# Attention of a two-layer encoder: three groups in rounds, value columns as weights, sums that come out transposed

## The reference

```python
# a: latent attention, head width 96 for q and k, 64 for v
p = softmax(q @ k.T * 96**-0.5);  o = p @ v
# b: windowed attention, +-128 tokens, a sink logit per head
e = exp(s - m); p = e / (sum(e) + exp(sink - m)); o = p @ v
# c: two maps of width 32 per head
p1 = softmax(q1 @ k1.T * 32**-0.5);  p2 = softmax(q2 @ k2.T * 32**-0.5)
o = (p1 - lam * p2) @ v
o = rms_norm(o, norm_g) * (1 - lambda_init)
x = x + g1 * (concat(a, b, c, d) @ w_out)
```

## Time and profile before

| | |
|---|---|
| median of 3 runs | 1745.44 us (1743.79 to 1755.22) |
| the profiled execution | 1747.51 us |
| its span in the trace | 1745.7 us |
| PE busy | 1387.3 us (79%) |
| DVE, ACT, POOL busy | 618.0, 369.3, 265.9 us |
| attention stage, layer 0 | 314.64 to 480.61 us |
| attention stage, layer 1 | 1145.35 us to some 166 us later |

### The profile page before, as it was taken

How to read it: one execution, slowest core, us unless ns; L and a number is a source line. 1 busy time by engine, 2 the same in 40 slices (tenths; PEclk the granted TensorE clock), 3 DMA queues, 4 the chain that set the end, 5 groups by cost and what they waited for, 6 DMA issues and landing times.

```text
span 1745.7 us, 18431 instructions
## 1 busy us (share of the span) xinstructions
PE 1387.3 (79%) x6748; PEld 787.5 (45%) x6748; DVE 618.0 (35%) x1444; ACT 369.3 (21%) x832; POOL 265.9 (15%) x250
## 2 busy tenths in 40 slices
PE   2789999898696768878778999988869778877841
PEld 0245646565443434444324465656544344444421
DVE  3461523358624212221136152335861431111111
ACT  0211111545402101111021111154530211111101
POOL 0000301000001333333200030100000134333311
PEclk9789999999898779999978999999989879999986
DMA  7611120441334499999961113045124449999942
GB/s 234 253 51 48 72 88 10 155 179 44 127 123 157 180 295 408 407 406 402 360 226 63 48 51 109 2 146 191 49 104 146 157 158 386 403 401 401 398 141 109
DMA packets 98152, 335.53 MB, mean 192 GB/s; under 512 B 28310, under 2 KB 33046, under 8 KB 72816
## 3 DMA queue, kind: packets, MB, share of 16 engines
q1 hardware_dynamic: 74688, 305.48, 44.8%
q0 software_dynamic: 15072, 16.85, 4.2%
q10 hardware_dynamic: 8304, 12.03, 2.0%
HBM read 324.04 MB, written 27.80 MB: 202 GB/s over the span
## 4 chain that ended last, share of the span: by engine, by line
PE 63%; DVE 13%; issue 9%; ACT 7%; DMA 4%; POOL 2%; SPq 1%; POOLq 0%; DVEq 0%; ACTq 0%
PE bank L458 57%; ACT pr_r L1212 2%; DMA big<-in_ada_w_dram 2%; PE bank L706 2%; PE bank L804 2%; DVE pr_r L1679 1%; DVE pr_r L1818 1%; DVE pr_r L1821 1%; ACT pr_r L1259 1%; DVE pr_r L1544 1%; PE bank L790 1%; PE bank L556 1%; POOL small L1319 1%; ACT ht_r L1191 1%; SPq L917 1%
## 5 line engine op out<-in xcount | busy, mean ns | idle before, releaser
L458 PE MATMUL bank<-big,pr_r 128*64 128x256 f32 (+2 forms) x3272 | 471.0, 407 | 103.6 <-issue 62.2
L458 PEld LDWEIGHTS bank<-big,pr_r 128*64 128x64 f32 (+1 forms) x3272 | 286.8, 152 | 260.5 <-issue 157.0
L458 PE MATMUL bank<-big,ht_r 128*128 128x512 f32 (+2 forms) x832 | 329.9, 547 | 1.4 <-ACT ht_r L1225 1.4
L458 PEld LDWEIGHTS bank<-big,ht_r 128*128 128x128 f32 x832 | 155.0, 190 | 144.5 <-issue 138.0
L458 PE MATMUL bank<-big 128*128 128x256 f32 (+4 forms) x528 | 189.8, 500 | 27.3 <-ACT big L1196 10.5
L1383 POOL DMA_INDIRECT x_rows<-ht_r,slot_i x64 | 101.7, 1590 | 364.7 <-DVE ht_r L1824 326.3
L458 PEld LDWEIGHTS bank<-big 128*128 128x128 f32 (+2 forms) x528 | 100.8, 202 | 84.4 <-issue 39.8
L1818 DVE TENSOR_TENSOR pr_r<-pr_r,bank 64x256 f32<-64x256 f32 x65 | 27.5, 423 | 295.7 <-ACT pr_r L1259 250.0
L1259 ACT ACTIVATE pr_r<-bank 64x256 f32<-64x256 f32 x64 | 24.1, 377 | 460.7 <-PE bank L458 420.5
L1824 DVE SCALAR_TENSOR_TENSOR ht_r<-bank,mix_r,mod 128x512 f32<-128x512 f32 x65 | 48.8, 751 | 135.7 <-PE bank L458 135.7
L1318 POOL TENSOR_SCALAR small<-small 128x1 f32<-128x1 f32 (+2 forms) x20 | 6.9, 346 | 574.9 <-DVE small L1704 326.7
(11 more groups left out here) (272 smaller groups left out, 1215.7 us busy)
## 6 DMA issues: line engine op xcount, KB each, us to landing
big<-in_moe_w_gate_dram SPq DMA_DIRECT2D x65, 1024.0 KB, 5.0
big<-in_moe_w_up_dram SPq DMA_DIRECT2D x65, 1024.0 KB, 7.0
big<-in_moe_w_down_dram SPq DMA_DIRECT2D x65, 1024.0 KB, 9.1
big<-in_ada_w_dram SPq DMA_DIRECT2D x16, 3072.0 KB
big<-in_w_in_dram SPq DMA_DIRECT2D x4, 3072.0 KB
big<-in_w_out_dram SPq DMA_DIRECT2D x4, 2048.0 KB
mod<-in_ada_b_dram SPq DMA_DIRECT2D x12, 512.0 KB, 5.1
big<-in_w_in_dram SPq DMA_DIRECT2D x2, 2048.0 KB
```

Source lines behind the costliest of these rows:

```text
L458: return nc.tensor.matmul(o, l, r, start=start, stop=stop)
```

## The change

- **Order.** The outs go in 16 rounds: one out of c, then two of a (rounds 1 to 8) or two of b (rounds 9 to 16); the two are of neighbouring heads and the same queries. S is given two outs ahead. `prob` and `probT` have six buffers. P comes after outs 11, 20, 27, 33 and 39. The banks are split four ways: three for the scores of a and c, two for transposes and P, two for the sums of PV, one for the scores of b and all the rest.
- **c on 32-row tiles.** The two maps of a head are two products over 32 rows each, on different row tiles, into different banks. b runs on 64-row tiles. The zero fills and the eight copies are gone.
- **PV.** The values of one head (64 columns) are the weight and `probT` is streamed; two heads lie side by side on two 64-column tiles. The sums come out transposed, 64 channels of two heads by 512 queries, one bank for 8 outs. Step E copies the bank to `mixT` (ACT) and inverts the row sums (DVE). Since a row sum now belongs to a column, step R spreads the inverses over a bank with eight products against `ident`, and DVE multiplies `mixT` by that bank. For c, ACT also squares the bank (`usq`), step Q sums over the channels with four two-column products, and POOL makes the factor for R.
- **End.** The final transposes of `mix_tok` and their copies are gone. `w_out` sums the blocks in another order: convolution first, then as they were closed. `gd` is loaded with two transfers instead of one.

The core of the diff:

```diff
-        prob, probT = at(pr_r, 0, 4, S), at(pr_r, 2048, 2, S)
+        prob, probT = at(pr_r, 0, 6, S), at(mix_r, 0, 6, S)
...
+        kinds = []
+        for r in range(NH * NT):
+            kinds += ["c"] + ["ab"[r // 8]] * 2
...
-        MOD_AFTER = {3: 3, 8: 4, 13: 5, 18: 6, 23: 7}
+        MOD_AFTER = {11: 3, 20: 4, 27: 5, 33: 6, 39: 7}
+        steps, later, pv_no, closed = [("S", 0), ("S", 1), ("K", 0)], [], {}, []
+        for k in range(len(outs) + 5):
+            if k < len(outs):
+                steps.append(("T", k))
+            if k + 2 < len(outs):
+                steps.append(("S", k + 2))
+            if k + 1 < len(outs) and outs[k + 1][0] == "c":
+                steps.append(("K", k + 1))
+            if 0 < k <= len(outs) and outs[k - 1][1] % 2:
+                g, o = outs[k - 1][:2]
...
+                steps.append(("PV", (g, o - 1)))
+                if o % 8 == 7:
+                    block = (g, o // 8)
+                    closed.append(block)
+                    steps.append(("E", block))
+                    later += [(k + 1, "Q", block), (k + 3, "R", block)] if g == "c" else [(k + 1, "R", block)]
+            steps += [(what, n) for when, what, n in later if when == k]
...
+            scores, turned, work, sums = (Products(pe, g, b) for g, b in (("s", (4, 5, 6)), ("t", (7, 0)), ("w", (1,)), ("o", (2, 3))))
...
                         elif g == "c":
-                            i = 2 * h + m
-                            mm(A.bank(f"S{n}")[:, :], qT_c[:, i, q], kT_c[:, i // 4, :]).then_inc(ready_a, 1)
+                            both = [scores.bank(f"S{m}") for m in ms]
+                            for i, b in enumerate(both):
+                                r = slice(32 * ((2 * h + i) % 4), 32 * ((2 * h + i) % 4) + 32)
+                                mm(b[:, :], qT_c[r, h // 2, q], kT_c[r, h // 2, :]).then_inc(ready_s, 1)
...
+                        for j, kt in enumerate(tiles):
+                            for i in range(2):
+                                last = mm(b[64 * i:64 * i + 64, qt * P:(qt + 1) * P], value[g](kt, h + i),
+                                          probT[:, at_out[g, o + i] % 6, j * P:(j + 1) * P], j == 0, j == len(tiles) - 1)
+                        last.then_inc(ready_o if qt == NT - 1 else pv_done, 1)
+                    elif what == "Q":
+                        taken(pe, f"Oc{n[1]}")
+                        b = work.bank(f"Q{n[1]}")
+                        for t in range(NT):
+                            last = mm(b[:, 2 * t:2 * t + 2], usq[:, t * P:(t + 1) * P], halves)
+                        last.then_inc(ready_w, 1)
+                    elif what == "R":
...
+                        for t in range(NT):
+                            for i in range(2):
+                                x = 8 * pair + 2 * t + i
+                                last = mm(b[64 * i:64 * i + 64, t * P:(t + 1) * P], r[:, x:x + 1].to_broadcast([P, 64]), ident[:, :])
...
-                pe.wait_ge(mix_ready, l + 1)
-                for j in range(6):
-                    b = A.bank(f"xT{j}")
...
-                act.wait_ge(padded, 2 * l + 2)
...
-                    for i in range(4):
-                        last = A_(qT_c[32 * i:32 * i + 32, 4 * j + i, :], b[32 * i:32 * i + 32, :], ACT.Copy,
-                                  scale=DIFF_SCALE)
+                    A_(qT_c[:, j, :], b[:, :], ACT.Copy, scale=DIFF_SCALE).then_inc(taken_a, 1)
...
+                for pair in range(2):
+                    mine = slice(8 * pair, 8 * pair + 8)
+                    g.wait_ge(dss_ready, 2 * l + pair + 1)
+                    step(rstd(drs[:, mine], dss[:, mine], 1.0 / 64))
+                    g.tensor_tensor(drs[:, mine], drs[:, mine], r_out[2][:, mine], ALU.mult).then_inc(drs_ready, 1)
```

More of the change, by code:

```diff
@@ L236, in trunk @@
         dss, drs = sm(16), sm(16)
+        r_out = [sm(16) for _ in range(3)]
         invf = sm(48)
@@ L378, in trunk @@
-        steps.append(("PV", len(outs) - 1))
+            g, n, _ = of(name)
+            eng.wait_ge(groups[g][1], n + 1)
+        kinds = []
+        for r in range(NH * NT):
+            kinds += ["c"] + ["ab"[r // 8]] * 2
+        outs, maps, seen = [], [], {"a": 0, "b": 0, "c": 0}
+        for g in kinds:
+            o = seen[g]
+            seen[g] += 1
+            outs.append((g, o, 2 * (o // 8) + o % 2, o % 8 // 2, list(range(len(maps), len(maps) + 1 + (g == "c")))))
+            maps += [len(outs) - 1] * (1 + (g == "c"))
@@ L380, in band, with used @@
+        mixed = [n for what, n in steps if what == "R"]
+        mix_block = {"a": 0, "b": 2, "c": 4}
+        assert len(closed) == len(mixed) == 6
+        def used(eng, k):
+            g, o = outs[k][:2]
+            if o % 8 >= 6:
+                done(eng, f"O{g}{o // 8}")
+            else:
+                before = [n for w, n in steps[:steps.index(("PV", (g, o - o % 2)))] if w == "PV" and n[1] % 8 < 6]
+                eng.wait_ge(pv_done, 18 * in_layer[0] + len(before) + 1)
         def band(n):
@@ L733, in layer @@
-                taken(pe, "xT5")
+                        mod_sum(n, work)
+                for group in (scores, turned, sums):
+                    group.all_taken()
                 for half in range(2):
@@ L738, in layer @@
                     for t in range(NT):
+                        if half == 0 and V.banks[V.n % 4] == 1:
+                            work.all_taken()
                         b = V.bank(f"w{half}{t}")
-                        for k in range(KT):
+                        order = [6, 7] + [mix_block[g] + pair for g, pair in mixed]
+                        for n, k in enumerate(order):
+                            if half == 0 and t == 0 and n >= 2:
+                                taken(pe, "R{}{}".format(*mixed[n - 2]))
                             src = mixT[:, k, t * P:(t + 1) * P] if k < 6 else ydT[:, k - 6, t * P:(t + 1) * P]
-                            last = mm(b[:, :], src, w[:, k, :], k == 0, k == KT - 1)
+                            last = mm(b[:, :], src, w[:, k, :], n == 0, n == KT - 1)
                         last.then_inc(ready_v, 1)
```

356 lines of the change are left out of this document (180 added, 176 removed).

## The result

The changed kernel takes 1824.53 us (median of 4 runs, 1814.89 to 1828.02), the kernel before 1744.62 us beside it: a ratio of 1.042, 95% interval 1.039 to 1.046. It is slower by 80 us, where 1742 was forecast and 1780 was the top of the range. The span of the profiled execution is 1823.5 us, 77.8 more than before.

The account below looks back on a forecast made before the run. PE streams a third less, but the chain from c's scores to its T (4.8 us) binds. Per layer −9.6 + 8 = −1.6, twice, plus 0.5: −2.7 from 1747.5, 1744.8; as median 1742 us, range 1700 to 1780.

Parts of the forecast that it names:

- The clock: Attention stage: waits of over 2 us lose 1.7 us at 1.2 GHz in half of ten intervals, plus 8 us a layer.
- the slow rival: PE stays at 1.2 GHz through the plain rounds, 3.8 us more each over ten intervals and two layers: 1803; chance 0.15.
- the fast rival: The clock stays at 2.4 GHz, a gain of 19 us: 1727; chance 0.17.
- Chain and waits: Scores of c to its T take 4.8 us or more; rounds average 8.1 (a) and 7.7 us (b), PE idling in each.
- Side by side: The two maps of c on row tiles take 0.87 us together, a pair of PVs on column tiles 0.9 instead of 1.75.
- The rival with row tiles in turn: Row tiles of c run one after the other, 0.75 us a round, 15 rounds, two layers: 1764; chance 0.10.
- P and M, 20.8 us: P/M in the stage cost 2.9 us twice (first half) and 5.0 three times (second half): 20.8, against 21 before.
- R and Q, 4.5: In the stage: R of a and b 0.7 us each, Q 0.4, two R's behind each other 2.6: 4.5.
- Entry, −4.4: Without the zero fill and with two copies for eight, PE starts 4.4 us earlier in each layer.
- Tail, 11.9: From the last T of c to `w_out` 11.9 us, against 17.55 before: minus 5.6 a layer.
- The round order gives nothing: First T to last T of c takes 144.0 us a layer, against 143.8 before; PE's saving turns into waiting.

Follow-up runs that it names:

- before_narrow: The kernel before, in its own order, with only b's scores on 64 rows and c's on 32 instead of 128: 1766.0 us, ratio 1.011.

## Why the prediction was wrong

Step by step, per layer. What the terms are without most of the loss of clock is read from the kernel with three unread products ("filled"), whose stage was granted 0.95.

- **The clock, "I take such a loss in half of them: plus 8 us"**: this is the step that failed. The stage took 207.8 us against 178.0 with the fill, and by my estimate the fill itself costs 5.6, since the two P of the a half, hidden in the wait before, now come beside it (P and M 5.7 instead of 2.9 a time). That leaves 207.8 − 172.4 = 35 us for the clock instead of 8: 27 of the 39 us by which a stage missed. The price of one fall, 1.7 us, was taken from an expert's products on all 128 rows, which were back at the higher clock before their end; here PE stays low for whole rounds. The sentence against the slow rival, "the busy stretches of 5 us between the waits should raise it again", was wrong for the rounds with b: 9.0 us of work between two waits, scores on 32 and 64 rows among them, stayed at the lower clock (435.19 to 444.18).
- **The slow rival** named the mechanism and gave 1803. Its price was right: a plain round with b takes 11.38 us and 7.53 in the filled kernel, 3.85 more, for 3.8; and its 38 us a stage stand beside the 35 measured. What it lacked are the 11.7 us a stage of the other terms below: 1803 + 23 = 1826. I gave it 0.15, because the busy stretches should raise the clock again. The condition that I wrote down for the fast rival, that b had waits before and kept 0.96, was weak evidence: those waits were 1.72 us at most (PE at 381.95), and soon behind that longest one PE's rows were at the lower clock (383.69). The 64 rows alone don't make the difference: in the old order b on 64 rows kept 0.93 in layer 0 of `before_narrow`.
- **Chain and waits**: right. Rounds of 7.81 against 7.7 and 7.53 against 7.3 at 2.4 GHz, waits of 1.95 to 2.71 us before 13 of the 16 T's of c, released by K.
- **Side by side**: right for c (1.13 us with drain against 0.87 streamed) and nearly so for PV: 16 instructions in 1.03 us to the next, against 0.9 and 0.1 for the change. The rival with row tiles in turn falls.
- **P and M, 20.8 us**: too low by 3.3 us. In the b half of the filled kernel the rounds with P and M take 14.1 us on average, the plain ones 8.0 (7.53 twice, and 8.89 with the R of b in it): 6.1 each for 5.0.
- **R and Q, 4.5**: too low by 1.3. The round with both R's takes 11.3 us, 3.4 over a plain one, and Q and the first R of a, in rounds before it, cost some 2.3. The forecast's own items add up to 4.4.
- **The rest of the 39 us**: the first round 3.7 (it has no fill and runs at the lower clock, 11.8 us for 8.1) and plain rounds 2. With P and M, R and Q and the tail that is 3.7 + 2 + 3.3 + 1.3 + 1.4 = 11.7, beside the clock's 27.4. How it divides between the small terms is my estimate; the sum is measured. The first round and part of the tail are the clock's too.
- **Entry, −4.4**: right, about −5 in both layers.
- **Tail, 11.9**: 13.3 in the filled kernel and 15.7 as it ran. POOL's power took 1.63, as taken (1.6). The two R's (1.98 each, with 0.94 between) were counted at the higher clock; behind PE's wait for POOL they run at the lower one in the filled kernel too.
- **"The round order gives nothing"**: first T to last T of c take 160.0 us in the filled kernel, 154.4 without the fill's 5.6, against 144.0 forecast and 143.8 before: the order loses some 10 us even there. And it was read as a tie when it meant that PE, with a third less to do, would stand idle in every round. The work that was removed had also kept the clock up.

The Trainium skill, TensorE: Matmul & The Clock Gate, A second HAM failure mode, says of a kernel that cycles through the banks of PSUM that short idle times between groups of products are frequent enough there to make the clock swing between its two levels. The traces agree for waits of 1.95 to 2.71 us.

What stays open: which of c's 32 rows and b's 64 weighs more per column, and whether 64-column tiles count in full; no kernel here changed the columns of PV alone. A product on fewer rows also brings a change of tile before and behind it (about 0.1 us each); no kernel separates that from the rows, though the filled kernel has all these changes and its b half was granted 1.00. Nor was it tried whether T, a transpose, holds the clock as a product does, though its share of PE's work grows when the rest falls. c's scores at full rows were tried only as sums over four maps, in the late order.

## What to carry to other kernels

Before taking work off TensorE, ask what it will wait for afterwards: where a chain on other engines sets the pace, the removed columns become idle time, and the lower clock then doubles what is left. Try a kernel with unread products in the wait; if it gets faster, the clock is the cause, and the cure is an order that puts real work there. Zero rows in a product cost PE no time here and may be worth keeping, because with them the clock stayed higher.

## What the runs showed of the hardware

- With waits of 1.95 to 2.71 us in 13 of 16 rounds, TensorE was granted 0.82 and 0.65 of its clock over two half stages; with three unread products in each wait it was 0.92 and 1.00, and the kernel 62 us faster.
- At the same instructions and columns, products on 32 rows were granted 0.64 and on 128 rows 0.82 of the clock over a half stage (52 us in the kernel's time), tile changes included; for b's scores 64 against 128 rows made 22, 11 and 34 us in three kernels.
- A PE without any idle time stayed at 1.2 GHz for 30 us in which 58% of its time went to products on 32 rows.
- Whether the clock is low can differ between two layers of one execution that run the same code (1.00 in the c part of `before_narrow`'s layer 0, 0.50 to 0.52 for 30 us at the start of that of layer 1); its four runs scatter by 22 us, the eleven of the kernel before beside it by 14.
- Two products of 32 rows on different row groups end together (1.13 us for both); two 64-column tiles take 0.13 us per pair of 128 columns at 2.4 GHz, 0.24 at 1.2.
